# Last mixer tile in halves of 512 columns, tile 6 placed sooner, first expert rows gathered inside the mixer

## The reference

```python
x = x + g1 * (mixed @ w_out[l])                       # "mixer": out-projection and residual
h2 = rms_norm(x, norm2_w[l]) * (1 + sc2) + sh2        # what the experts read
logits = h2 @ w_router[l] + b_router[l]               # 32 experts
top_logits, top_idx = lax.top_k(logits, 4)            # 4 experts for each token
top_w = softmax(top_logits)
# each expert e, over the tokens that chose it:
gu = xe @ w_gate_up[e] + b_gate_up[e]
y  = activation(gu) @ w_down[e] + b_down[e]
x  = x + g2 * (sum over the 4 experts of top_w * y)
```

## Time and profile before

| what | us |
|---|---|
| median of 3 runs (lowest, highest) | 2389.32 (2388.61, 2389.77) |
| the profiled execution, its own time | 2392.84 |
| span of that execution in the trace | 2391.2 |
| TensorE busy, of the span | 2255.1 (94%) |
| VectorE busy | 1742.3 (73%) |
| ScalarE busy | 1293.0 (54%) |
| GpSimd busy | 794.3 (33%) |

### The profile page before, as it was taken

One profiled execution on the slowest core, in us unless ns is written; L12 is line 12 of the kernel. 1 busy time (PEld: TensorE's weight loads), 2 busy tenths in 40 slices (PEclk: granted clock), 3 DMA queues, 4 the chain that ended last, 5 costly groups with the idle time before them and its releaser, 6 DMA issues.

```text
span 2391.2 us, 37523 instructions
## 1 busy us (share of the span) xinstructions
PE 2255.1 (94%) x10570; PEld 1819.6 (76%) x10571; DVE 1742.3 (73%) x2124; ACT 1293.0 (54%) x1736; POOL 794.3 (33%) x784
## 2 busy tenths in 40 slices
PE   6899997888976999999999999999999999999997
PEld 2679876776764788888878888878888887878886
DVE  1684423577765799976689866687999768689697
ACT  2332212675324677755567655566777556576575
POOL 2153003792234233432223222232333322233242
PEclk9899998899987999999999999999999999999999
DMA  7134205882235899987689967697999868799695
GB/s 245 61 128 146 59 17 131 249 224 78 106 115 200 288 370 372 372 290 232 215 283 373 361 216 231 224 321 241 368 378 361 302 215 276 261 330 371 230 352 176
DMA packets 299220, 583.98 MB, mean 244 GB/s; under 512 B 23889, under 2 KB 53601, under 8 KB 297057
## 3 DMA queue, kind: packets, MB, share of 16 engines
q1 hardware_dynamic: 269248, 501.68, 60.2%
q0 software_dynamic: 26560, 69.06, 10.6%
q10 hardware_dynamic: 3362, 12.59, 1.4%
HBM read 544.79 MB, written 44.24 MB: 246 GB/s over the span
## 4 chain that ended last, share of the span: by engine, by line
PE 62%; DVE 4%; issue 2%; DVEq 1%; DMA 0%; ACT 0%; ACTq 0%; POOL 0%; POOLq 0%
PE psum L2036 55%; DVE d_wlo L1863 3%; PE psum L2018 3%; PE psum L1976 2%; PE psum L1986 2%; DVE d_up L1876 0%; DMA d_xg<-xn_d,d_entry 0%; DVE d_act L1882 0%; DMA d_entry<-list_d 0%; DVE d_atlo L1888 0%; DVEq L1542 0%; DVE d_y_two L1853 0%; DVEq L1541 0%; ACT d_y_two L1764 0%; DVEq L1540 0%
## 5 line engine op out<-in xcount | busy, mean ns | idle before, releaser
L1863 DVE TENSOR_TENSOR d_wlo<-d_raw,d_whi 128x1024 fp32r<-128x1024 f32 x578 | 673.8, 1218 | 81.5 <-ACT d_whi L1739 79.9
L1739 ACT ACTIVATE d_whi<-d_raw 128x1024 fp32r<-128x1024 f32 x578 | 574.6, 1053 | 117.8 <-PE psum L2036 86.0
L2036 PE MATMUL psum<-d_whi,d_xthi 128*128 128x512 f32 x1152 | 458.7, 398 | 0.1
L2036 PE MATMUL psum<-d_whi,d_xtlo 128*128 128x512 f32 x1152 | 454.6, 395 | 0.0
L2036 PE MATMUL psum<-d_wlo,d_xthi 128*128 128x512 f32 x1152 | 454.5, 394 | 0.0
L1863 DVE TENSOR_TENSOR d_wlo<-slab,d_whi 128x1024 fp32r<-128x1024 f32 x292 | 343.5, 1218 | 15.4 <-ACT d_whi L1739 13.6
L1642 POOL DMA_INDIRECT out_dram<-d_yst,d_dest x49 | 93.3, 1905 | 781.5 <-DVE d_yst L1910 724.8
L1739 ACT ACTIVATE d_whi<-slab 128x1024 fp32r<-128x1024 f32 x292 | 292.5, 1054 | 6.0 <-PE psum L2036 5.6
L2036 PEld LDWEIGHTS psum<-d_whi,d_xtlo 128*128 128x128 f32 x1152 | 217.0, 188 | 50.7
L2036 PEld LDWEIGHTS psum<-d_whi,d_xthi 128*128 128x128 f32 x1152 | 217.0, 188 | 50.0 <-issue 1.6
L2036 PEld LDWEIGHTS psum<-d_wlo,d_xthi 128*128 128x128 f32 x1152 | 217.2, 189 | 48.3
(11 more groups left out here) (322 smaller groups left out, 3984.4 us busy)
## 6 DMA issues: line engine op xcount, KB each, us to landing
slab<-in_w_gate_up_dram SPq DMA_DIRECT2D x144, 1024.0 KB
d_raw<-in_w_gate_up_dram SPq DMA_DIRECT2D x144, 1024.0 KB, 9.0
d_raw<-in_w_down_dram SPq DMA_DIRECT2D x144, 1024.0 KB, 7.1
b_wp<-in_w_ada_dram POOLq DMA_DIRECT2D x16, 1024.0 KB, 7.7
slab<-in_w_in_dram SPq DMA_DIRECT2D x12, 1024.0 KB, 5.5
slab<-in_w_ada_dram SPq DMA_DIRECT2D x8, 1024.0 KB
a_xin<-in_x_dram ACTq DMA_DIRECT2D x2, 2048.0 KB
v_d<-a_vst POOLq DMA_DIRECT2D x16, 256.0 KB, 2.7
```

Of the source, the lines that this page charges most:

```text
L1739: nc.scalar.activation(whi[n % NW][:, part, :], raw[n % NRAW][:, part, :], ACT.Copy).then_inc(whi_ok, 1)
L1863: nc.vector.tensor_tensor(wlo[n % NW][:, part, :], raw[n % NRAW][:, part, :], whi[n % NW][:, part, :].bitcast(F32), ALU.subtract).then_inc ...
L2036: mm = nc.tensor.matmul(to, m_[:, KH * h + k, :], w_[n % NW][:, k, :], start=(h == 0 and k == 0 and q == 0), stop=(h == 1 and k == KH - 1 ...
```

## The change

- The last tile (7) goes in halves of 512 columns through residual, squares, norm, transposes, copy and logits. The first half's residual and squares are done while TensorE is still projecting the second half. The root takes both partial sums (ScalarE). Tile 7's logits go to PSUM bank 1 in place of bank 7.
- Tile 6: VectorE's `choose(6)` stands ahead of `norm2(7)` instead of behind it, and TensorE's `positions(6)` ahead of tile 7's transposes instead of behind its logits.
- Tile 7's store of x + residual is issued behind its root instead of ahead of its squares.
- GpSimd's mixer program now ends with the two entry loads and the two gathers of the first group. The expert block no longer has them. To make that possible, `entry` and `xg` live outside the blocks (`xg` in `modacc`, two unused quarters of it); the zeroing of the lower half of `xg[1]` moves to GpSimd's program behind the scatters of tile 1; the experts' `sg`, `up` and `yst` buffers of 128 rows also lie in `modacc`.

```diff
@@ mixer, GpSimd
+                    if i == 1:
+                        pool.wait_ge(bc_mm, 4)
+                        own.link(nc.gpsimd.memset(xg[1][P // 2:, :], 0.0))
                 for b in range(2):
                     pool.wait_ge(list_st[b], 16 * K4 * NT // 2)
+                for b, rows in enumerate((P, P // 2)):
+                    pool.dma_start(s.entry[b][:, :], s.list_d[b * P:b * P + rows, :]).then_inc(s.entry_in[b], 16)
+                for b in range(2):
+                    pool.wait_ge(xn_st[b], 16 * NT // 2)
+                for b, rows in enumerate((P, P // 2)):
+                    pool.wait_ge(s.entry_in[b], 16)
+                    if b:
+                        pool.wait_ge(table_ok, 1)
+                    pool.indirect_dma_start(out=xg[b][0:rows, :], out_offset=None, in_=s.xn_d[:, :],
+                                            in_offset=bass.IndirectOffsetOnAxis(ap=s.entry[b][:, 0:1], axis=0)
+                                            ).then_inc(s.xg_in[b], 16)
@@ mixer, ScalarE
+                    if last(i):
+                        act.wait_ge(h2_half, 1)
+                        nc.scalar.activation(h2T[b][:, 0:KT // 2, :].rearrange("p k n -> p (k n)"), psum[:, 5, :],
+                                             ACT.Copy).then_inc(h2_half_ok, 1)
                     act.wait_ge(xn2_ok, i + 1)
                     act.dma_start(s.xn_d[bass.ds(i * P, P), :], xn2[b][:, :]).then_inc(xn_st[b], 16)
...
+                def last_square(i, b):
+                    act.wait_ge(x1_half, 1)
+                    act.wait_ge(ssq2, i)
+                    nc.scalar.activation(dump[:, 0:SL], xt[b][:, 0:SL], ACT.Square,
+                                         accum_out=st[b][:, 3:4]).then_inc(ssq2, 1)
+                    act.wait_ge(x1_ok, i + 1)
+                    act.wait_ge(ssq2, i + 1)
+                    nc.scalar.activation(dump[:, SL:D], xt[b][:, SL:D], ACT.Square,
+                                         accum_out=st[b][:, 7:8]).then_inc(ssq2, 1)
+                    act.wait_ge(ssq2, i + 2)
+                    act.wait_ge(half_ok, 1)
+                    nc.scalar.activation(st[b][:, 4:5], st[b][:, 7:8], ACT.Sqrt, bias=st[b][:, 6:7],
+                                         scale=1.0 / D).then_inc(xrs_ok, 1)
+                    act.dma_start(s.out[bass.ds(i * P, P), :], xt[b][:, :]).then_inc(x1_st[b], 16)
@@ mixer, VectorE
+                def last_residual(i, b):
+                    dve.wait_ge(y_half, 1)
+                    dve.wait_ge(xn_st[b], 8 * (i - b))
+                    dve.wait_ge(x_in[b], 8 * (i - b) + 16)
+                    for h in range(2):
+                        cols = slice(h * SL, (h + 1) * SL)
+                        if h:
+                            dve.wait_ge(ssq2, i + 1)
+                            nc.vector.tensor_scalar(st[b][:, 6:7], st[b][:, 3:4], 1.0 / D, EPS,
+                                                    ALU.mult, ALU.add).then_inc(half_ok, 1)
+                            dve.wait_ge(y_mm, i + 1)
+                        nc.vector.tensor_tensor(xn2[b][:, cols], psum[:, 2 * b + h, :], gate1[:, cols],
+                                                ALU.mult).then_inc(gated, 1)
+                        dve.wait_ge(gated, i + 1 + h)
+                        nc.vector.tensor_tensor(xt[b][:, cols], xn2[b][:, cols], xt[b][:, cols],
+                                                ALU.add).then_inc(x1_ok if h else x1_half, 1)
...
                     if there(t - 2):
                         place(t - 2, b)
+                    if last(t):
+                        choose(t - 1, 1 - b)
                     if there(t):
                         norm2(t, b)
-                    if there(t - 1):
+                    if there(t - 1) and not last(t):
                         choose(t - 1, 1 - b)
@@ mixer, TensorE
+                    if last(t - 1):
+                        positions(t - 2, b)
                     if there(t - 1):
                         turn_norm(t - 1, 1 - b)
...
-                    if there(t - 2):
+                    if there(t - 2) and not last(t - 1):
                         positions(t - 2, b)
@@ experts
-                for b in range(2):
-                    pool.dma_start(entry[b][:, :], s.list_d[b * P:b * P + ROWS[b], :]).then_inc(entry_in[b], 16)
-                own.link(nc.gpsimd.memset(xg[1][HB:, :], 0.0))
...
-                for b in range(2):
-                    gather(b, 0, True)
                 setup()
```

More of the change, by code:

```diff
@@ L97, in shared @@
     s.ident_r = sb("ident_r", [P, P], F32R)
+    s.entry = [sb(f"entry{b}", [rows, 3], I32) for b, rows in enumerate((P, P // 2))]
+    s.entry_in, s.xg_in = ([nc.alloc_semaphore(name=f"{n}{b}") for b in range(2)] for n in ("entry_in", "xg_in"))
     s.psum = ctx.enter_context(nc.psum_tensor("psum", [P, 8, 512], F32))
@@ L1027, in there, with last, logit_bank @@
             return not isinstance(t, int) or 0 <= t < NT
+        def last(t):
+            return isinstance(t, int) and t == NT - 1
+        def logit_bank(i):
+            return 1 if last(i) else 7
         def past(t, n):
@@ L1231, in norm2 @@
                     own.link(nc.vector.reciprocal(row[:, 5:6], row[:, 4:5]))
+                    if last(i):
+                        for h in range(2):
+                            cols = slice(h * SL, (h + 1) * SL)
+                            own.link(nc.vector.scalar_tensor_tensor(xn2[b][:, cols], xt[b][:, cols], row[:, 5:6],
+                                                                    gain2[:, cols], ALU.mult, ALU.mult))
+                            nc.vector.tensor_tensor(xn2[b][:, cols], xn2[b][:, cols], shift2[:, cols],
+                                                    ALU.add).then_inc(xn2_ok if h else xn2_half, 1)
+                        return
                     own.link(nc.vector.scalar_tensor_tensor(xn2[b][:, :], xt[b][:, :], row[:, 5:6], gain2[:, :],
@@ L1386, in project @@
                                                       start=(kt == 0 and q == 0), stop=(kt == KT - 1 and q == 2))
+                        if last(i) and j == 0:
+                            mm.then_inc(y_half, 1)
                     if piece:
@@ L1390, in turn_norm @@
                 def turn_norm(i, b):
-                    pe.wait_ge(xn2_ok, i + 1)
+                    if not last(i):
+                        pe.wait_ge(xn2_ok, i + 1)
                     if past(i, 1):
@@ L1399, in logits @@
                 def logits(i, b):
-                    pe.wait_ge(h2_ok, i + 1)
+                    if last(i):
+                        pe.wait_ge(h2_half_ok, 1)
+                    else:
+                        pe.wait_ge(h2_ok, i + 1)
                     if past(i, 1):
@@ L1403, in logits @@
                     for k in range(KT):
-                        mm = nc.tensor.matmul(psum[:, 7, 0:E], h2T[b][:, k, :], wr[:, k, :],
+                        if last(i) and k == KT // 2:
+                            pe.wait_ge(h2_ok, i + 1)
+                        mm = nc.tensor.matmul(psum[:, logit_bank(i), 0:E], h2T[b][:, k, :], wr[:, k, :],
                                               start=(k == 0), stop=(k == KT - 1))
```

37 lines of the change are left out of this document (27 added, 10 removed).

## The result

The changed kernel takes 2397.07 us (median of 9 runs, 2393.11 to 2402.24) beside 2389.32 of the kernel before (9 runs, 2387.04 to 2394.30) on the same chip. The ratio is 1.0029, 95% interval 1.0018 to 1.0040: slower by about 7 us by the ratio (7.75 by the medians), where 2386.9 was forecast, and outside the range given. The profiled execution's own time is 2395.94 us, 1.64 above its span.

What follows compares the result with a forecast made beforehand. TensorE's unbroken matmuls from 751 us were taken as the bound, so only their start counted: 2.85 us later and 5.3 less made -2.45. Taking 2.4 from the median 2389.32 gave 2386.9 us, whole range 2384.5 to 2391.5.

Steps and rivals of the forecast that it cites:

- What bounds the kernel: TensorE's matmuls run without a hole from 751 us; the change is worth only what it moves their start.
- part 2: Entry loads and gathers now stand ahead of GpSimd's DRAIN, taken as 2.67 us; the DRAIN's end comes 2.85 us later.
- Part 1: Mixer's end, tiles 6 and 7: tile 7's scatters start 2.9 us sooner, and the scatters' end moves as much.
- The rival in which the reordering does nothing: GpSimd stays behind with tile 6 in the mixer; costs the 2.9 us gain and gives 2389.8 us; chance 0.05.
- the rival's 3.94: Moved transfers no quicker: entry load takes 3.94 us, the step behind it 0.86, 2.1 + 0.5 more; 2389.5 us; chance 0.2.
- the faster rival: 128-row gather issues in 0.94 us, DRAIN takes 1.44, logits run half at their faster pace; 2383.6 us; chance 0.12.
- The slower rival: GpSimd's DRAIN waits for the gathers in flight, then takes 2.67 us, ending at 732.9; 2391.5 us; chance 0.15.
- Part 3: Behind the DRAIN's end, no wait for the gather: the way to the bias matmul is 5.3 us less.
- Sum: +2.85 - 5.3 = -2.45 us: the bias matmul starts at about 748.6.
- the same: Whole kernel within about 0.2% (4.8 us) of the kernel before; chance 0.84.

Runs made afterwards that it cites:

- e5: The changed kernel unaltered, run again on another chip, gap 64: 2396.78 us, ratio 1.0023 to the kernel before.
- e10: The changed kernel plus 64 unused bytes between the split weights and the buffers behind them, gap 128: 2390.62 us, ratio 1.0000 to the kernel before.
- e8: The kernel before plus the mixer's halves, tile 6 sooner and only the entry loads in the mixer, gap 64: 2392.80 us, ratio 1.0007.
- e13: e8 with 64 unused bytes that put the expert buffers where the kernel before has them, gap 128: 2387.33 us, ratio 0.9981 to the kernel before.
- e17: The kernel before plus 192 unused bytes between the split weights and the buffers behind them, gap 64: 2394.31 us, ratio 1.0014.
- e3: The kernel before plus only tile 7 by halves and tile 6 sooner, loads and buffers as before, gap 128: 2386.90 us, ratio 0.9989.
- e9: e4 plus a wait for both gathers to land ahead of GpSimd's DRAIN, gap 128: 2397.60 us in one run.
- e2: The changed kernel with weights and stationary rows at the addresses of the kernel before, gap 128: 2392.26 us, ratio 1.0007 to the kernel before.
- e4: The changed kernel with the weights' 64-byte shift taken back, stationary rows still about 8 KB lower, gap 128: 2389.40 us, ratio 1.0003 to the kernel before.
- e18: e8 plus 192 unused bytes ahead of the experts' small buffers, gap 0: 2361.50 us, ratio 0.9876 to the kernel before.
- e15: The kernel before plus 128 unused bytes between the split weights and the buffers behind them, gap 0: 2364.28 us, ratio 0.9887.
- e12: The kernel before with 64 unused bytes ahead of the stationary buffers and 64 behind them, gap 192: 2377.72 us, ratio 0.9949.
- e19: The changed kernel plus 192 unused bytes between the split weights and the buffers behind them, gap 0: 2362.51 us, ratio 0.9890 to the kernel before.

## Why the prediction was wrong

**What bounds the kernel.** Right that TensorE's matmuls without a hole set the time. The step that failed is the sentence drawn from it: "The change touches nothing in that long part except the place of some buffers, so it can be worth only what it moves the start of that part." The place of some buffers was put at nothing. It is worth 4.4 us by the pace, and by pairs of kernels that differ in the gap alone (64 and 128) 5.5 by e5 against e10 (1.0023 and 1.0000), 6.2 by e8 against e13 and 3.3 by e17 (1.0014, interval 1.2 to 5.5 us). The even loss after 775 us in the changed kernel, e17 (loss without the change) and e10 (change without the loss) show it. No rival held it. That is the larger step; the smaller is the DRAIN in part 2.

**The starts, compared cleanly.** The time at which the mixer ends drifts by some us between executions, so I count from the end of the last projection matmul of the mixer (695.57 before, 695.15 after), read off TensorE's timeline:

| from there to | before | after | e3 | e13 |
|---|---|---|---|---|
| tile 6's first scatter | 15.65 | 10.29 | 10.29 | 10.29 |
| tile 7's first scatter | 20.75 | 17.63 | 17.63 | 17.62 |
| DRAIN's end (D) | 29.80 | 35.27 | 26.92 | 28.75 |
| first bias matmul | 55.49 | 55.60 | 51.31 | 51.57 |

The last line is 54.1 to 55.8 in six profiles whose mixer is that of before (mean 54.9) and 55.2 to 56.4 in eight of the full change without e9's wait (mean 55.7).

**Part 1** forecast tile 7's scatters 2.9 us sooner; it is 3.12. The step is right. Their end was to move as much, but the wait for them is over only 2.4 to 2.9 us sooner (the changed kernel, e3). e3 by itself has D 2.88 sooner, and a median 3.0 lower with an interval that touches zero. The rival in which the reordering does nothing is out: e3's bias matmul starts 51.31 behind the mixer's end, before 54.1 to 55.8.

**Part 2** forecast D 2.85 later; it is 5.47. The entries landed in 1.9 to 2.0 (1.8 taken; the rival's 3.94 is out). The gathers came 0.9 later than written, at 723.0: the entries' issue started 0.3 later (720.21 for 719.9), the landing took 0.15 more, and the step from landing to gather took 0.84. The prediction took 0.4 for it, putting the 0.86 of before down to a semaphore step that the moved code doesn't have; here the rival had its 0.5 right. The two gather issues took 2.28, and not 3.33: this part of the faster rival came true. The mis-sized term is the DRAIN: taken as 2.67, it measured 7.12, of which 1.98 lie beside the gathers' issue. The slower rival had the mechanism, a wait for the gather in flight, and then 2.67, for D = 732.9. It had the flight too long (5.58; e2 and e4 show 4.6 to 4.8 for the same transfers), and some 1.5 us and not 2.67 follow the landing. So D was 730.42. That is just short of the rival's turning point of 730.7 in the page's time, and just past it counted from the mixer's end (5.47 against 5.3).

**Part 3** forecast 5.3 us less behind D. From D to the bias matmul it was 25.69 and is 20.33: 5.36 less. The path is the one written down as well: the low part of the turned rows is done at 739.11 + 1.28 = 740.39, which is D + 9.97 (9.95 forecast).

**Sum.** The start was to come 2.45 us sooner and comes 0.1 later than in the profile before, 0.8 later by the means. With the pace's 4.4 to 6 that makes 5 to 7 us; measured 7.0 (4.3 to 9.6). Against the forecast, the start came 2.5 to 3.2 us too late, and the pace took the rest. At a gap of 128 the full change gives ratios of 1.0007, 1.0003 and 1.0000 (e2, e4, e10), so the forecast "the same" would have held for the order alone, though not its time: 2.4 less was forecast, 0 to 1.7 more found. What the halves gain, the gathers ahead of the DRAIN lose. TensorE's granted clock also differs between the profiles at the start of the row of matmuls: it moves between its two levels, 1.2 and 2.4 GHz, and 0.66 is the mean of a stretch that has both. The stretch view of before, then of after:

```profile
750.00:754.00 4.00, 2.86 (x6) 2.01 (x7) 3.84 (x5) 0.00 (x0) 2.01 (x2) 0.66 0.01 2
```
```profile
750.00:754.00 4.00, 3.05 (x12) 2.27 (x13) 3.53 (x5) 0.00 (x0) 2.54 (x4) 1.00 0.02 4
```

At 0.66 the first piece of eight matmuls takes 3.45 us, at 1.00 it takes 2.10. With the 0.3 us by which the bias matmul is sooner, that is why the changed kernel is 1.6 us ahead at 775. e3, with the old order of the loads, has the lower clock (3.50), and so do e4 and e9, with the new one, so I put these 1.4 us down to no part of the change.

**A kernel that beats both.** e18 (halves, tile 6 sooner, entry loads in the mixer, gathers behind the barrier, gap 0) takes 2361.5, 1.2% less than before. Nearly all of it is the gap: e15, the kernel before with 128 empty bytes, takes 2364.28. What the early entry loads add can't be told from zero: e13 gains 2.6 us by the medians where the halves alone (e3) gain 3.0, by the ratios it is 4.5 and 2.6, and the bias matmul starts 51.2 to 52.0 behind the mixer's end in the four kernels that have them, 51.31 in e3.

## What to carry to other kernels

When a kernel that is bound by back-to-back matmuls moves by some tenths of a per cent, compare the start-to-start time of the same matmuls before looking for a wait, and give any edit that moves buffers a twin with an empty buffer that puts them back. Here the distance between the moving and the stationary buffer was worth over ten times what the planned change could give, so its residues are worth a try early. Work moved ahead of a block's end must have landed by then: here GpSimd's DRAIN waited for the gathers in flight, so issuing early wasn't finishing early.

## What the runs showed of the hardware that I had not expected

- **The pace goes by the address gap of the two operands, modulo 256 bytes**: 227.4 ns at 0 (three kernels), 229.9 to 230.4 at 192 (four), 232.4 at 128 (eight), 233.1 at 64 (five). The order isn't monotonic, and the residues of the weights alone or of the rows alone don't sort the times: weights at 96 are found at all four gaps. That the period is 256 and not 512 is seen at one gap alone: 64 in e17 and 320 in the changed kernel give the same pace. The kernels at 0, at 128 and at 192 agree modulo 512 too. The matmuls are fp32r, 128x512, each with a weight load, while VectorE, ScalarE and DMA write the same memory. Why the gap matters, a conflict between the read of the moving operand and that of the next stationary one for instance, was only thought of and not tried; gaps between these four weren't either. The Trainium skill, "TensorE: Matmul & The Clock Gate", Step-by-step, has the two operands come through two independent read ports. Taken alone, that would leave the gap without a cost; e12, which moved the stationary rows by 64 bytes and gained 0.5%, doesn't agree.
- **GpSimd's DRAIN depends on what it issued and on what is in flight.** 1.44, 2.67 and 6.24 us in the earlier trace rows, behind 17, 32 and 67 transfers issued by GpSimd in the block. In e9, four more than in e3 make 3.0 of 2.67, and where these four have left the expert block the DRAIN at its end is shorter by as much, 4.56 in place of 4.88: some 0.08 us for each. It is no plain proportion, as that last DRAIN stands behind some 290. With two entry loads in flight it is 3.56, with two gathers in flight 7.0 to 7.25 in all eight kernels that have them.
- **The kernel's own spread is wide.** Executions of one kernel lie up to 5 us from their median, two up to 7 (e15, e19), so effects of 3 us took eleven runs a side to show, and not every one did (e3).
